# TensorE's order inside the attentions: the next head's logits of a token tile ahead of the running head's values

## What is computed

```python
def window_attention(q, k, v, sink, rel_table):   # first block: 16 query heads, 4 key/value heads, head dim 64
    ...
    logits = jnp.einsum('bnqgrd,bnkgd->bngrqk', qb, kb).astype(jnp.float32) * (ATTN_HEAD_DIM ** -0.5)
    ...
    logits = jnp.where(valid[None, :, None, None], logits + bias, -jnp.inf)
    ...
    m = jnp.maximum(jnp.max(logits, axis=-1, keepdims=True), sink_l)
    p = jnp.exp(logits - m)
    p = p / (jnp.sum(p, axis=-1, keepdims=True) + jnp.exp(sink_l - m))
    out = jnp.einsum('bngrqk,bnkgd->bnqgrd', p.astype(v.dtype), vb)
```

## Time and profile before

| | |
|---|---|
| median of 3 runs | 1844.65 us (1844.26 to 1845.07) |
| the profiled execution | 1842.23 us, of which the span is 1840.4 us |
| TensorE busy | 1804.4 us, 98% of the span |
| VectorE, ScalarE, GpSimd busy | 859.7, 828.9, 838.9 us (47%, 45%, 46%) |
| granted TensorE clock | 0.998 of full speed |
| DMA | 159.91 MB, mean 87 GB/s |

### The profile page before, as it was taken

How to read it: one execution, slowest core, us unless ns; L and a number is a source line. 1 busy time by engine, 2 the same in 40 slices (tenths; PEclk the granted TensorE clock), 3 DMA queues, 4 the chain that set the end, 5 groups by cost and what they waited for, 6 DMA issues and landing times.

```text
span 1840.4 us, 26869 instructions
## 1 busy us (share of the span) xinstructions
PE 1804.4 (98%) x9072; PEld 1499.2 (81%) x9072; DVE 859.7 (47%) x1409; ACT 828.9 (45%) x1764; POOL 838.9 (46%) x595
## 2 busy tenths in 40 slices
PE   8999999999999999999999999999999999999998
PEld 7788888888788788888888888887888888787876
DVE  4678888888404454234341044050063311344754
ACT  4655555455325655334432233253533442456652
POOL 4654555577353131445454455445364444542322
PEclk9999999999999999999999999999999999999999
DMA  5732212111133131333233233324232223221111
GB/s 177 136 94 63 64 58 67 57 58 58 58 103 120 35 109 41 106 124 97 92 91 103 92 94 100 102 82 160 80 105 90 82 91 95 89 84 58 58 47 58
DMA packets 46227, 159.91 MB, mean 87 GB/s; under 512 B 4763, under 2 KB 7195, under 8 KB 45884
## 3 DMA queue, kind: packets, MB, share of 16 engines
q1 hardware_dynamic: 38592, 140.53, 24.2%
q10 hardware_dynamic: 7548, 18.20, 4.0%
HBM read 152.42 MB, written 6.29 MB: 86 GB/s over the span
## 4 chain that ended last, share of the span: by engine, by line
PE 84%; DVE 7%; issue 4%; ACT 3%; POOL 1%; DMA 0%; DVEq 0%; ACTq 0%; POOLq 0%
PE main L301 61%; PE main L329 6%; PE aux L803 4%; PE main L1853 2%; PE aux L657 2%; PE aux L790 2%; DVE u_acc L2052 1%; PE aux L773 1%; PE aux L373 1%; PE aux L774 1%; DVE y_all L2130 1%; PE aux L1942 1%; PE aux L648 1%; DVE x_res L565 1%; ACT dmat L1367 1%
## 5 line engine op out<-in xcount | busy, mean ns | idle before, releaser
L264 POOL TENSOR_TENSOR w_lo<-raw,w_hi 128x512 fp32r<-128x512 f32 x504 | 705.5, 1408 | 867.8 <-ACT w_hi L260 862.3
L260 ACT ACTIVATE w_hi<-raw 128x512 fp32r<-128x512 f32 x486 | 303.6, 629 | 680.6 <-PE main L301 671.7
L301 PE MATMUL main<-w_hi,a_hi 128*128 128x512 f32 x736 | 304.7, 414 | 2.3 <-ACT vv L1597 1.5
L301 PE MATMUL main<-w_hi,a_lo 128*128 128x512 f32 x736 | 288.2, 392 | 0.0
L301 PE MATMUL main<-w_lo,a_hi 128*128 128x512 f32 x736 | 287.2, 390 | 0.0
L301 PE MATMUL main<-a_hi,w_hi 128*128 128x512 f32 x576 | 231.0, 401 | 1.9 <-ACT u_raw L1350 1.6
L301 PE MATMUL main<-a_hi,w_lo 128*128 128x512 f32 x576 | 225.0, 391 | 0.0
L301 PE MATMUL main<-a_lo,w_hi 128*128 128x512 f32 x576 | 224.5, 390 | 0.0
L301 PEld LDWEIGHTS main<-w_hi,a_lo 128*128 128x128 f32 x736 | 138.1, 188 | 30.2
L301 PEld LDWEIGHTS main<-w_hi,a_hi 128*128 128x128 f32 x736 | 138.5, 188 | 28.8 <-ACT vv L1597 1.9
L301 PEld LDWEIGHTS main<-w_lo,a_hi 128*128 128x128 f32 x736 | 138.9, 189 | 22.9
(11 more groups left out here) (323 smaller groups left out, 3113.1 us busy)
## 6 DMA issues: line engine op xcount, KB each, us to landing
raw<-w_stream_in SPq DMA_DIRECT2D x264, 512.0 KB, 3.5
x_res<-x_in ACTq DMA_DIRECT2D x8, 512.0 KB, 5.2
rel_rows<-rel_row ACTq DMA_DIRECT2D x1, 4096.0 KB, 44.3
bias<-rel_rows ACTq DMA_DIRECT2D x2, 1536.0 KB, 7.8
out<-x_res SPq DMA_DIRECT2D x4, 512.0 KB, 2.6
bgate<-b_gate_in ACTq DMA_DIRECT2D x4, 256.0 KB, 5.3
ln_g<-ln_g_in ACTq DMA_DIRECT2D x1, 1024.0 KB, 4.7
ln_b<-ln_b_in ACTq DMA_DIRECT2D x1, 1024.0 KB, 6.8
```

Source lines behind the costliest of these rows:

```text
L260: eng.activation(w_hi[:, k, :], raw[:, k, :], ACT.Copy).then_inc(hi_done, 1)
L264: eng.tensor_tensor(w_lo[:, k, :], raw[:, k, :], w_hi[:, k, :].bitcast(F32), ALU.subtract).then_inc(lo_done, 1)
L301: mm = eng.matmul(mb[m][:, :], lhs, rhs, start=(first and k == 0 and n == 0), stop=(last and k == KT - 1 and n == 2))
```

## The change

Inside `heads`, in what follows the three passes of a tile, the logits of head t+1 are issued first and the values of head t-1 second:

```diff
@@ -1865,10 +1865,10 @@
                             att.pe_turn_p(pe, j, t - 1, m)
 
                     def after(m):
+                        if t < 7:
+                            att.pe_logits(pe, j, t + 1, m, og)
                         if t:
                             att.pe_values(pe, j, t - 1, m)
-                        if t < 7:
-                            att.pe_logits(pe, j, t + 1, m, og)
                     h, l = op(t)
                     main_step(pe, p + 1, t, h, l, False, og + 1, before=before, after=after)
```

## The result

The changed kernel takes **1825.05 us** (median of 4 runs, 1824.69 to 1825.51) against 1844.45 us for the kernel before (4 runs, 1843.92 to 1845.07): ratio 0.9896, 95% interval 0.9882 to 0.9910. The profiled execution took 1824.98 us.

The account below looks back on a forecast made before the run. TensorE, busy 98%, sets the pace, so only array holes can be won. First attention's 7.8 and second's 6.5 us made 14.3 us; 1842.2 - 14.3 = 1827.9, with 2.4 us for the runs' median 1830.3 us, range 1826.0 to 1838.5.

Parts of the forecast that it names:

- The bound and the place: TensorE, busy 98%, sets the pace; only array holes count, at the values' weight loads (line 803), 124 waits, 37.7 us.
- the prediction's whole purse: All holes at the 124 waits of the values' loads in both attentions: 37.7 - 124 x 0.16 = 17.9 us.
- The reading of the holes: Values' loads: idle is about 0.16 us larger than the hole; holes 0.28, 0.16, 0.05, second attention 0.39, 0.05 us.
- The loop picture: Steady tile: logits leave the transposes-copy-values loop (1.84 us); TensorE's work of 2.04 us sets the pitch, before 2.20.
- What does not close: Turn from step 1 to 2: ScalarE limits, 0.23 of 0.57 us won; step 7's tile 0: 0.17 of 0.28, 0.38 of 0.39.
- The transposes now follow the values: Swapped tiles: transposes follow values instead of logits, costed at nothing, bounded by 0.03 us either way, 96 x 0.03 = 3 us.
- rival 4: Everything closes, step 1's turns too: 16.4 us, 1828.2 us; chance 0.80 together with the forecast.
- Rival 1: Full-weight loads are never hidden, so 0.11 us after each wait stays: 7.5 us won, 1837.1 us; chance 0.14 with half covers.
- Rivals 2 and 3: 2: time returns elsewhere, some 1843 us, chance 0.04; 3: values stand behind logits' wait on VectorE, 1852.4 us, chance 0.02.

Follow-up runs that it names:

- the second occasion: The unaltered changed kernel run again beside the kernel before on one chip: 1824.95 us against 1842.34 us, ratio 0.9905.

## Why the prediction came out as it did

- **The bound and the place: right.** The gain lies in the four loops: 17.8 us there, 17.25 us between the two profiled executions. But holes were not all that could be won: 17.8 us is the prediction's whole purse (17.9), and 37 idle loads are still there.
- **The reading of the holes: right.** An idle load of 0.32 us is a hole of 0.16; in steps 3 to 6 every pitch fell by at least its hole: 0.32, 0.20, 0.19 and 0.09 us for 0.28, 0.16, 0.16 and 0.05, and in the second attention 0.40 and three times 0.09 to 0.10 us for 0.39 and 0.05.
- **The loop picture: right**, and shown by the longer copy: where a tile waits for the copy, the unswapped order pays the added 0.12 us in full, and the swapped one none of it. The steady tile takes 2.00 us, where 2.04 were forecast.
- **What does not close: right in kind.** Step 2's turn is ScalarE's (shown by both kernels that feed it earlier), and the two tiles there earned 0.30 us together for 0.23 forecast. Step 7 earned 0.17 us in the first attention as written, 0.36 for 0.38 in the second.
- **The step that failed** is "The transposes now follow the values ... I cost it at nothing, bounded by 0.03 us either way". What the runs showed in its place is 0.03 to 0.05 us a tile (0.01 in tile 0 of the second attention), 3.5 us over the 96 tiles: a step from 3 to 6 earns 0.80 instead of 0.65 us and 0.68 instead of 0.54, and the loops 17.8 instead of 14.3. Both experiments that put a logits' matmul or a pass behind the values again, without a hole, bring back 0.04 to 0.05 us. I could have read it beforehand. At step 7 of the kernel before, the transposes follow the values:

```profile
637.71 0.74 PEld L803 LDWEIGHTS aux<-v_sb,pt 128*128 128x128 f32 x6 [0.32 <-ACT pt L886]
...
638.43 0.50 PE L790 MATMUL aux<-const,pr 128*128 128x128 f32 x3
```

  Six values take 638.43 - (637.71 + 0.11) = 0.61 us there. In the steady tile before, the second logits matmul starts at 631.03, and one of 384 columns takes 0.17 us (626.23 to 626.40 in the changed kernel), so the first took its place in the array at 630.86: 630.86 - (630.08 + 0.11) = 0.67 us. The pitches say the same: tile 1 takes 2.20 us in steps 3 to 6 and 1.80 at step 7, 0.40 us less, of which the two logits are 0.35. I took the 0.66 us of six loads for the values' own time, in the loop too, where 0.61 belonged.
- **The forecast and the range.** The forecast lies 5.25 us above the result. 3.5 us of it is the neighbourhood, less the 0.5 us that was lost outside the loops. The other 2.3 us come from the 2.4 us by which the median of before stood above its profiled execution and which I added. They were scatter of the executions: in the changed kernel the median (1825.05) is the profiled time (1824.98), and on the second occasion the median of before was 1842.34. The range's lower end was to take in rival 4 (1828.2) and 3 us of the unknown, which is 1825.2, and I wrote 1826.0; even 1825.2 would have been too high by 0.15 us.
- **Rival 1, the load that is never hidden: refuted.** The values' load starts at 626.41 while the second logits matmul (626.40, 384 columns) is running, and the tile earns its hole in full: its pitch is 2.00 us, where the rival had 2.1 or more. The rule of the Trainium skill (TensorE: Matmul & The Clock Gate, "Part 3: Packing small matmuls", The mechanism), that a load overlaps matmuls in flight only in other rows of the array, taken by itself does not hold for these loads of all 128 rows. By the rival 7.5 us would have been won; 17.8 were.
- **Rivals 2 and 3** did not come: of the 17.8 us some 0.5 were given back outside the loops, and logits wait for VectorE 6 times for 2.2 us, 0.6 at most. **Rival 4** did not come either: the turn to step 2 keeps its wait for the copy.

What stays open: why a transpose's load may follow the values' last load by 0.05 us and a logits' or pass's load only by 0.11. I had put it down to a shorter load of the transposes (0.14 us against 0.19). But directly behind the values their load is recorded with 0.20 us, as here in the changed kernel's second attention, so the records don't bear this out:

```profile
1684.68 0.20 PEld L790 LDWEIGHTS aux<-const,pr2b 128*128 128x128 f32 x1
```

## What to carry to other kernels

Where an in-order engine waits for a copy of its own result, take everything out of the loop result, copy, use that doesn't belong to it, and put it in front of the use: independent work after the wait lengthens the loop, the same work before it is cover. Then look at whose load or latency each instruction now hides or shows; here the same instructions in another succession were worth 3.5 us, a quarter of what was forecast for the holes. And a pattern that already exists elsewhere in the trace (here the step without logits) gives the price of the new neighbourhood before anything is run.

## What the runs showed of the hardware that was not expected

Six matmuls of 64 columns with weights of their own (the values of three key blocks) took 0.61 us to the start of a transpose behind them (626.59 to 627.20 in the changed kernel), and 0.67 us where a float32r matmul (logits) followed, by the working above, without any wait in between; the next load started 0.05 us behind the last in the first case and 0.11 us in the second, before a pass as before logits. The runs of the same kernel scatter by 3.3 us (before: 1841.75 to 1845.07 over both occasions), while the tile pitches in steps 3 to 6 of the changed kernel repeat to 0.01 us between its two profiled executions.
